# Another order of the three products of split units, one per layer, mixer and FFN loop, with whole-unit release in two of them

## The reference, cut to what matters

```python
# first block, layer i
out = merged @ w_o
r = ALPHA * x + out
r = r + jax.nn.sigmoid(r @ w_pg) * (p_i @ w_p)
...
# second block
def hybrid_mixer(h, w_in, ...):
    proj = h @ w_in
...
def swiglu(h, w_gate, w_up, w_down):
    return (jax.nn.silu(h @ w_gate) * (h @ w_up)) @ w_down
```

## Time and profile before

| | us |
|---|---|
| median of 2 runs | 2161.74 (2158.09 and 2165.39) |
| the profiled execution | 2157.13 |
| its span | 2155.2 |
| TensorE busy in it | 2122.2 |
| GpSimd busy in it | 655.2 |

### The profile page before, as it was taken

One profiled execution on the slowest core, in us unless ns is written; L12 is line 12 of the kernel. 1 busy time (PEld: TensorE's weight loads), 2 busy tenths in 40 slices (PEclk: granted clock), 3 DMA queues, 4 the chain that ended last, 5 costly groups with the idle time before them and its releaser, 6 DMA issues.

```text
span 2155.2 us, 33529 instructions
## 1 busy us (share of the span) xinstructions
PE 2122.2 (98%) x13296; PEld 1889.9 (88%) x13296; DVE 1418.1 (66%) x1430; ACT 1294.6 (60%) x1428; POOL 655.2 (30%) x318
## 2 busy tenths in 40 slices
PE   9999999999999999999999999999999999999998
PEld 8979999988999898999998888888888888888886
DVE  1455223346413694223696999999998989999997
ACT  4546444455644554434554777777777777777775
POOL 6717785825788202888401000000000000000000
PEclk9999999999999999999999999999999999999999
DMA  7434554515455343555455999999999999999994
GB/s 241 136 92 160 176 180 150 186 56 169 155 186 181 101 132 118 195 184 186 140 177 169 377 377 336 373 355 376 358 350 368 363 377 343 359 354 371 366 362 184
DMA packets 307359, 529.03 MB, mean 245 GB/s; under 512 B 11826, under 2 KB 152786, under 8 KB 307248
## 3 DMA queue, kind: packets, MB, share of 16 engines
q1 hardware_dynamic: 306512, 526.44, 69.8%
q0 software_dynamic: 736, 1.00, 0.2%
HBM read 525.84 MB, written 1.05 MB: 244 GB/s over the span
## 4 chain that ended last, share of the span: by engine, by line
PE 86%; POOL 5%; DVE 4%; ACT 2%; issue 2%; DMA 0%; POOLq 0%; DVEq 0%; ACTq 0%
PE bank L701 84%; POOL weights_low L2866 5%; PE bank L1386 1%; DVE qb L2150 1%; ACT sc L1499 1%; DVE sc L2150 1%; PE bank L869 0%; DVE sc L2158 0%; PE bank L772 0%; ACT weights_high L1502 0%; DVE h L2158 0%; DVE nmax L2185 0%; ACT sq L1499 0%; ACT expert_weights_high L1502 0%; DVE y L2158 0%
## 5 line engine op out<-in xcount | busy, mean ns | idle before, releaser
L2150 DVE TENSOR_TENSOR expert_weights_low<-ring_experts,expert_weights_high 128x2048 fp32r<-128x2048 f32 x336 | 764.7, 2289 | 73.2 <-ACT expert_weights_high L1502 73.0
L1502 ACT ACTIVATE expert_weights_high<-ring_experts 128x2048 fp32r<-128x2048 f32 x336 | 644.0, 1917 | 168.6 <-PE bank L701 163.7
L2866 POOL TENSOR_TENSOR weights_low<-ring,weights_high 128x1024 fp32r<-128x1024 f32 x254 | 620.9, 2467 | 375.9 <-ACT weights_high L1502 375.7
L1502 ACT ACTIVATE weights_high<-ring 128x1024 fp32r<-128x1024 f32 x294 | 303.6, 1056 | 339.3 <-PE bank L701 305.5
L701 PE MATMUL bank<-x_high,weights_high 128*128 128x256 f32 x1024 | 288.8, 285 | 0.9 <-POOL weights_low L2866 0.9
L701 PE MATMUL bank<-x_high,weights_low 128*128 128x256 f32 x1024 | 282.8, 279 | 0.0
L701 PE MATMUL bank<-x_low,weights_high 128*128 128x256 f32 x1024 | 280.1, 283 | 0.0
L701 PE MATMUL bank<-h_high,weights_high 128*128 128x256 f32 x704 | 198.1, 284 | 5.3 <-ACT h_high L1502 5.3
L701 PE MATMUL bank<-h_high,weights_low 128*128 128x256 f32 x704 | 196.8, 282 | 0.0
L701 PEld LDWEIGHTS bank<-x_high,weights_low 128*128 128x128 f32 x1024 | 194.3, 190 | 0.1
L701 PEld LDWEIGHTS bank<-x_high,weights_high 128*128 128x128 f32 x1024 | 192.3, 188 | 2.3 <-DVE zs L2158 1.3
(11 more groups left out here) (320 smaller groups left out, 3831.3 us busy)
## 6 DMA issues: line engine op xcount, KB each, us to landing
ring_experts<-in_moe_w_gate_dram SPq DMA_DIRECT2D x112, 1024.0 KB, 6.9
ring_experts<-in_moe_w_up_dram SPq DMA_DIRECT2D x112, 1024.0 KB, 6.8
ring_experts<-in_moe_w_down_dram SPq DMA_DIRECT2D x112, 1024.0 KB, 6.5
ring<-in_w_in_dram SPq DMA_DIRECT2D x62, 1024.0 KB, 5.2
ring<-in_w_merge_dram SPq DMA_DIRECT2D x24, 1024.0 KB, 5.2
ring<-in_w_out_dram SPq DMA_DIRECT2D x14, 1024.0 KB, 5.2
ring<-in_ffn_w_gate_dram SPq DMA_DIRECT2D x11, 1024.0 KB, 5.2
ring<-in_ffn_w_up_dram SPq DMA_DIRECT2D x11, 1024.0 KB, 5.2
```

What stands on the lines that cost most here:

```text
L1502: return nc.scalar.activation(dst, src, ACT.Copy, scale=scale)
L2150: return nc.vector.tensor_tensor(dst, x, z, op)
L2866: nc.gpsimd.tensor_tensor(half_of(wlo[:, q_slot, :], t, width), half_of(ring[:, slot, :], t, width), half_of(whi[:, q_slot, :], t, width). ...
```

## The change

`split_project` gets a parameter `order`. The calls of layer 0 pass "two_phases", those of layer 1 "phases", those of mixer 0 "there_and_back", those of mixer 1 "low_first" and those in the FFN loop "by_tile"; the head of the FFN keeps the old order. In "two_phases" and "by_tile" the unit waits for both low halves at its start, and `used` and `count` are counted at its last two products.

```diff
-            def split_project(b, slot, lo_at, x, count):
+            def split_project(b, slot, lo_at, x, count, order="high_first"):
 
                 wh, wl = (w[:, slot, :].rearrange("p (k n) -> p k n", n=S) for w in (whi, wlo))
+                begun = [False, False]
+
+                def part(t, kk, w, xp):
+                    ins = mm(views(b)[:, t, :], w[:, kk, t * P:(t + 1) * P], x[xp][:, kk, :],
+                             not begun[t] and (both is False or t == 0), False, share=True)
+                    begun[t] = True
+                    return ins
+
+                both = order in ("two_phases", "by_tile")
+                if both:
+                    pe.wait_ge(lo_done.h, lo_at + 1)
+                    for kk in range(DT):
+                        for t in (0, 1):
+                            last = part(t, kk, wh, 0), part(t, kk, wl, 0)
+                        if order == "by_tile":
+                            for t in (0, 1):
+                                last = part(t, kk, wh, 1)
+                                if kk == DT - 1 and t == 0:
+                                    last.then_inc(used.h, 1)
+                    if order == "two_phases":
+                        for kk in range(DT):
+                            for t in (0, 1):
+                                last = part(t, kk, wh, 1)
+                                if kk == DT - 1 and t == 0:
+                                    last.then_inc(used.h, 1)
+                    last.then_inc(count.h, 1)
+                    return
                 for t in range(2):
                     pe.wait_ge(lo_done.h, lo_at + t)
-                    cols = slice(t * P, (t + 1) * P)
                     for kk in range(DT):
-                        mm(views(b)[:, t, :], wh[:, kk, cols], x[0][:, kk, :], kk == 0, False)
-                        mm(views(b)[:, t, :], wh[:, kk, cols], x[1][:, kk, :], False, False)
-                        ins = mm(views(b)[:, t, :], wl[:, kk, cols], x[0][:, kk, :], False, kk == DT - 1)
+                        if order == "phases":
+                            part(t, kk, wh, 0)
+                            ins = part(t, kk, wl, 0)
+                        elif order == "low_first":
+                            part(t, kk, wl, 0)
+                            part(t, kk, wh, 0)
+                            ins = part(t, kk, wh, 1)
+                        elif order == "there_and_back":
+                            for w, xp in ((wl, 0), (wh, 0), (wh, 1))[::1 if kk % 2 else -1]:
+                                ins = part(t, kk, w, xp)
...
+                    if order == "phases":
+                        for kk in range(DT):
+                            ins = part(t, kk, wh, 1)
                     ins.then_inc((used if t == 0 else count).h, 1)
...
-                        split_project(begin(name), *take_split(name, (mh, ml)))
+                        split_project(begin(name), *take_split(name, (mh, ml)), ("two_phases", "phases")[layer])
...
-                            split_project(begin(name), *take_split(name))
+                            split_project(begin(name), *take_split(name), ("two_phases", "phases")[layer])
...
-                        split_project(begin(name), *take_split(full2))
+                        split_project(begin(name), *take_split(full2), ("there_and_back", "low_first")[m])
...
-                        split_project((u + 2) % 4, (q0 + u) % 2, lo_at, (hh, hl), ff_full)
+                        split_project((u + 2) % 4, (q0 + u) % 2, lo_at, (hh, hl), ff_full, "by_tile")
```

More of the change, by code:

```diff
@@ L710, in split_project @@
                 for t in range(2):
                     pe.wait_ge(lo_done.h, lo_at + t)
-                    cols = slice(t * P, (t + 1) * P)
                     for kk in range(DT):
-                        mm(views(b)[:, t, :], wh[:, kk, cols], x[0][:, kk, :], kk == 0, False)
-                        mm(views(b)[:, t, :], wh[:, kk, cols], x[1][:, kk, :], False, False)
-                        ins = mm(views(b)[:, t, :], wl[:, kk, cols], x[0][:, kk, :], False, kk == DT - 1)
+                        if order == "phases":
[8 more added lines that the diff above has]
+                                ins = part(t, kk, w, xp)
+                        else:
+                            part(t, kk, wh, 0)
+                            part(t, kk, wh, 1)
+                            ins = part(t, kk, wl, 0)
```

## The result

The changed kernel takes 2181.20 us (two runs, 2180.84 and 2181.57) against 2161.74 before. The ratio on record is 1.0104, with a 95% interval of 1.0084 to 1.0123; the quotient of these two medians alone would be 1.0090, because one of the two runs of the kernel before, 2165.39, is longer than any of its ordinary runs beside the experiments. Four more runs of the changed kernel gave 2181.28 and a ratio of 1.0112 (1.0094 to 1.0130). With 15 and 19 runs the kernel before has medians of 2158.1 and 2158.3, so that the loss is 23 us, 1.1%: no change by the measure of 2%, on the slow side, 6 us above the forecast of 2175 and inside its range. What follows shows that the 6 us are a sum of errors of both signs.

A forecast was written before the change was run, and what follows sets the result against it. TensorE, busy 98% of the span, was taken as the bound. Layer 0 waits 16.7, loop 2.0 and pace -2.4 sum to 16.3 on 2157.13, 2173.4; with 1.6 for the median, 2175 us, range 2163 to 2188.

The forecast's parts named there:

- dk0: Layer 0 unit: its second high half stands behind exps(0) on ScalarE, so TensorE starts at 71.0 against 67.97; wait 3.0 us.
- step B of batch 5: Layer 0 attention: mg2's half 0 waits for mg0's end, so exps(5) starts 2.72 later; nothing covers it, 2.7 us.
- the cycle of a slot: Release to next low weights, GpSimd's two halves taken as 4.75: 6.18 against 5.68 us, so TensorE waits 0.50 every second unit.
- az1 with cz0: Layer 0: waits of 1.22 and 2.36 us, not added because VectorE's backlog absorbs the first; taken 2.4, otherwise 1.2 more.
- the rival on the clock: Low-clock windows in mixer 0 or 1, shifted in time, may be none or two: 3.7 us either way; no separate chance.
- 0.04 per unit: Pace gain in us for each of 60 units on x in both layers: -2.4 us in all; units on h nothing.
- The adjacency rival: Three orders never reuse a weight tile in adjacent products: 118 to 188 ns each, 276 us, 2450; chance 0.02.
- 2.0 us for unit 2: FFN loop: one wait of 0.5 us per iteration, four iterations; bounds nothing to 4 us.
- Unit 3 of the loop starts without a wait: FFN loop, a named sign: only every second changed unit waits, since the preceding 0.5 us wait gives this one time.
- The rule that I set aside: VectorE with two SBUF inputs and GpSimd exclude each other for whole instructions; dk0 would cost up to 5.9, not 3.0.
- rival 1: Queues on ScalarE make it worse: four more layer 0 softmax chains pay 2.7 each, az1's 1.2, dk0 2.9 more; 2190, chance 0.12.
- Rivals 2 and 3: Second: attention's waits shrink, half of 16.7 goes, 2162, chance 0.10. Third: weight loads no longer hidden, 2450, chance 0.02.

The follow-up runs named there:

- experiment 6: Changed kernel with ScalarE's order mended in layer 0: both high halves after dq0 ahead of exps(0), exps(5) ahead of both at mg0; 2172.69 us, ratio 1.0060.

## Why the prediction was right, and where it was not

**Layer 0's waits: right in mechanism, term by term.** Each term stands against what it measured (idle of the timeline plus 0.16 each, less what was there before): aq1, ak1 and av1 2.1, measured 1.01 + 0.21 + 0.21 + 0.48 = 1.9; dk0 3.0, measured 3.0; mc0 1.05, measured 0.9; step B of batch 5 2.7, measured 3.31 - 0.47 = 2.8; mg4 to mg11 2.7, measured 2.9; ou2 to pg3 2.8, measured 2.6. The wait "at every second unit" is as the cycle of a slot said. The step that failed is az1 with cz0, "I do not add the two": both waits stood in full, 0.95 + 0.16 and 3.10 - 0.44, 3.8 and not 2.4. The sum of the waits is 17.9 against 16.7.

The reason given was that VectorE, ahead of exps(4), does not wait for TensorE there. It did not, but it waited for GpSimd. Its product into y has two SBUF operands, and GpSimd's half for a later unit follows TensorE, through ScalarE. These are the two before:

```profile
164.87 2.37 POOL L2866 TENSOR_TENSOR weights_low<-ring,weights_high 128x1024 fp32r<-128x1024 f32 x1 [1.08 <-ACT weights_high L1502]
166.49 1.84 DVE L2158 SCALAR_TENSOR_TENSOR y<-zs,y 128x1024 f32<-128x1024 f32 x1
```

and in the changed kernel:

```profile
173.24 2.36 POOL L2906 TENSOR_TENSOR weights_low<-ring,weights_high 128x1024 fp32r<-128x1024 f32 x1 [2.15 <-ACT weights_high L1542]
173.77 2.91 DVE L2198 SCALAR_TENSOR_TENSOR y<-zs,y 128x1024 f32<-128x1024 f32 x1
```

VectorE reaches y 7.28 later (173.77 against 166.49), so up to there az1's wait was absorbed, as predicted. GpSimd's half starts 8.37 later, with all of TensorE's delay. In both traces y ends 1.1 us behind the end of that half (168.33 behind 167.24, 176.68 behind 175.60), so y ends 8.35 later, and so do exps(4), the split of cz0 and its low half (185.81 against 177.46 in the earlier trace rows). This is a reading of two traces, the same in the second profile of the changed kernel and in experiment 6 (y takes 2.98 and 2.85 there); no run took an operand of y out of SBUF.

**The clock: wrong.** "The longest new waits ... are like the 2.64 us without a product in the window at 840, where the clock stayed at 1.00." At dk0 and step B of batch 5 it fell to 1.2 GHz behind 2.9 and 3.3 us without products, in both profiles of the changed kernel, and cost 3.4 us by the estimate; the runs with zeros ahead of the wait show for dk0 and cz0 that the lack of products was the cause. In the rival on the clock I had only moved the falls that were there, and never let a new wait make one. From mixer 1 on the low clock made 3.0 more, which that rival's 3.7 either way covered. With the pace about 2 us (units of 5.54 to 5.62 where 5.71 stood, and some of 5.73, with a slower first product behind a wait), layer 0 comes to 17.9 + 3.4 - 2 = 19.3 of the measured 19.6.

**The pace: right in sign, a third of its size.** 0.04 per unit came from pg0's 5.66, the only unit of the new kind on x that was read. Measured are 0.12, so that layer 1 is 3.2 us shorter and not 1.2, nor within the "0 to 1.5" named as a sign; why pg0 was slower than the changed units, no run tells. Nothing for units on h was right, and the mixers' 0 too. The adjacency rival (2450) has no support.

**The loop: half.** 2.0 us for unit 2 was right (34.55 - 34.08 = 0.47 per iteration once VectorE is out of the way). "Unit 3 of the loop starts without a wait" was wrong: 34.97 - 34.08 = 0.89 per iteration, 3.6 in all. What failed is the 4.75 for a pair of halves in the cycle of a slot: beside VectorE the pair took 5.20. The other 0.5 of the FFN's 4.1 is at the head of mixer 1, where TensorE waits for h_high, in the chain behind a load of parameters (q): 1.75 to 1.91 us in the six profiles with by_tile and VectorE as it was, 1.41 with by_tile and the value in PSUM, 1.06 to 1.36 in the seven others. The forecast has no term for it, and no run took it apart.

**The rule that I set aside.** The earlier trace rows have GpSimd's half at 2.84 to 2.89 instead of 2.40, and I read 0.4 to 0.5 as the whole of what VectorE can cost. The other side of the same meeting was in the trace of the kernel before: VectorE's hidden_low takes 2.90 where GpSimd started 0.04 ahead of it and took its plain 2.39:

```profile
907.80 2.90 DVE L2150 TENSOR_TENSOR hidden_low<-hf,hidden_high 128x512 fp32r<-128x512 f32 x1
```

```profile
907.76 2.39 POOL L2866 TENSOR_TENSOR weights_low<-ring,weights_high 128x1024 fp32r<-128x1024 f32 x1 [0.44 <-ACT weights_high L1502]
```

907.76 + 2.39 = 910.15, and 0.55 of work is left to 910.70. So hidden_low isn't long; it waits for GpSimd and then works 0.55, and a half of GpSimd that comes directly behind must wait for that: 5.20 - 4.77 = 0.43 in the loop. The Trainium skill, page "SBUF — State Buffer", section "SBUF: two separate sides", says just this: the one that starts first has the ports for its whole instruction. The trace agrees, in the loop and at y above, and the run with the value in PSUM shows it (GpSimd's pair 4.77 and not 5.20). What I got right was dk0's 3.0 (GpSimd's half took 2.69 there); what I got wrong was to give the rule a price of 2.9 from VectorE rows that were themselves waits, to reject it with that price, and then not to ask where else a pair of halves behind each other meets VectorE: unit 3 of the loop was one such place, y was another. In the old loop the halves stood 0.45 apart and the meeting cost nothing.

**The total.** 16.3 forecast, +1.2 waits, +3.4 clock in layer 0, +3.0 clock further on, +2.1 for the FFN with the head of mixer 1 (4.1, where 2.0 was forecast), -0.8 and -2.0 pace in the two layers: 23.2, of 23.6 by the spans. So the 2175 came near by luck in part: terms of 1 to 3 us were missed on the one side, and the gain of the pace was sized too small on the other. The 1.6 us added for the median stand outside this sum; with more runs the kernel before has its median 1.0 to 1.2 above the profiled execution. Of rival 1 one part came, az1's 1.2, which reached cz0 after all; its four further softmax chains did not (behind B of batch 5 no step B waits longer than before), nor did dk0 cost more. Rivals 2 and 3 had no part: nothing was eaten, and nothing was slower by 2%.

## What to carry to other kernels

In this kernel a release that moved from the middle of a unit to its end cost twice: a small wait at every second unit, and a large one wherever the engine it releases has something else queued between the halves. Move that queue with it; two calls put in another place on ScalarE gave back 9 of 23 us here, 5.4 of them in layer 0 itself. A faster order of products should keep the release where it was: "phases" in both layers is the best of these kernels, 0.9968 of the time before. And where two engines meet, read the row of each: a long instruction on one of them may be a wait for the other, and carry its delay into a chain that seemed free of it, as y did here.

## What the hardware did that I had not expected

- A VectorE subtraction of 128x512 with two SBUF operands took 2.78 to 2.90 us beside GpSimd, and 0.69 with one operand in PSUM. The normalising products of the softmax (sc<-sc,pinv, two instructions) took 1.82 with GpSimd idle and 4.03 with GpSimd at work:

```profile
64.54 4.03 DVE L2150 TENSOR_TENSOR sc<-sc,pinv 128x1024 f32<-128x1024 f32 x2
...
114.85 1.82 DVE L2150 TENSOR_TENSOR sc<-sc,pinv 128x1024 f32<-128x1024 f32 x2
```

- The pace of products on x hangs on their order (5.59 to 5.61 or 5.70 to 5.71 us for 48). On h and merged no difference was seen: 34.07 and 34.08 us for an iteration of the loop, 22.8 for the four ou units.
- TensorE's granted clock fell to 1.2 GHz behind waits of 2.86 and 3.31 us and did not fall behind another of 3.10 in the same execution; with the old order and the late release it fell behind 2.70 and 3.01 and not behind 3.15. Ten products with zeros ahead of the wait kept it up.
